# Two blocks of a transformer and a state space model on one core: the norms' root, reciprocal and spread in two halves of 64 columns

## What is computed

```python
def layer_norm(x, g, b):                       # four times: n = 0, 1, 2, 3
    mu = jnp.mean(xf, axis=-1, keepdims=True)
    var = jnp.mean(jnp.square(xf - mu), axis=-1, keepdims=True)
    return (xf - mu) * lax.rsqrt(var + LN_EPS) * g + b

def rmsnorm(x, g):                             # three times: n = 4, 5, 6
    return xf * lax.rsqrt(jnp.mean(xf * xf, axis=-1, keepdims=True) + RMS_EPS) * g

for i in range(2):                             # first block
    ...                                        # attention and retention, both gated
    x = layer_norm(ALPHA * x + merged @ w_out[i], ...)             # n = 0, 2
    x = layer_norm(ALPHA * x + conv_glu_ffn(x) + sigmoid(x @ w_ple_gate[i]) * (p[i] @ w_ple_proj[i]), ...)   # n = 1, 3
u = rmsnorm(x, norm_mix) @ w_in                # second block, n = 4
h = x + mixed(u) @ w_out
h = h + swiglu(rmsnorm(h, norm_ffn))           # n = 5
out = rmsnorm(h, norm_final)                   # n = 6
```

## Time and profile before

| | us |
|---|---|
| median of three runs | 2319.66 |
| lowest and highest | 2319.19, 2320.61 |
| the profiled execution, its own time | 2319.28 |
| its span in the trace | 2317.4 |
| TensorE (PE) busy in the span | 2287.2 (99%) |
| VectorE (DVE), ScalarE (ACT), GpSimd (POOL) busy | 962.9, 973.4, 1149.2 |

### The profile page before, as it was taken

The page is one execution under the profiler, slowest core; times in us unless marked ns, Lnnn a source line. Parts: engine busy times, 40 slices in busy tenths (PEclk is TensorE's granted clock), DMA queues, the critical chain, the costliest instruction groups (busy, mean ns, idle before and its releaser), DMA issues.

```text
span 2317.4 us, 32473 instructions
## 1 busy us (share of the span) xinstructions
PE 2287.2 (99%) x11672; PEld 1890.9 (82%) x11672; DVE 962.9 (42%) x1611; ACT 973.4 (42%) x1372; POOL 1149.2 (50%) x702
## 2 busy tenths in 40 slices
PE   8999999999999999999999999999999999999998
PEld 7888888888888887888888888888888777888886
DVE  6355343344444204453553353334376774222201
ACT  5444443244555325444453243555512534443321
POOL 3433334578995455333334465444455666444452
PEclk9999999999999999999999999999999999999999
DMA  5222223322223422222222323233333213233321
GB/s 208 77 67 88 79 80 101 100 85 93 91 93 106 135 92 84 70 88 79 78 83 91 100 83 100 91 100 100 100 103 107 65 38 109 91 100 100 99 92 55
DMA packets 61284, 214.18 MB, mean 92 GB/s; under 512 B 7200, under 2 KB 7456, under 8 KB 61216
## 3 DMA queue, kind: packets, MB, share of 16 engines
q1 hardware_dynamic: 58336, 205.10, 27.9%
q10 hardware_dynamic: 2880, 8.15, 1.1%
HBM read 211.13 MB, written 2.10 MB: 92 GB/s over the span
## 4 chain that ended last, share of the span: by engine, by line
PE 94%; DVE 3%; POOL 1%; ACT 1%; issue 1%; DMA 0%; DVEq 0%; ACTq 0%
PE psum L825 85%; PE psum L853 2%; PE psum L854 2%; PE psum L858 2%; PE psum L956 1%; PE psum L944 1%; PE psum L923 1%; POOL run L774 1%; PE psum L1223 0%; DVE states L2241 0%; PE psum L1012 0%; PE psum L1049 0%; DVE pr L1886 0%; POOL run L780 0%; POOL u_all L783 0%
## 5 line engine op out<-in xcount | busy, mean ns | idle before, releaser
L459 POOL TENSOR_TENSOR w_lo<-stage,w_hi 128x1024 fp32r<-128x1024 f32 x378 | 926.3, 2459 | 1070.7 <-ACT w_hi L1369 1055.8
L825 PE MATMUL psum<-xh,w_hi 128*128 128x512 f32 x1712 | 671.2, 392 | 0.7 <-DVE scaled L2366 0.7
L825 PE MATMUL psum<-xl,w_hi 128*128 128x512 f32 x1712 | 666.9, 390 | 0.0
L825 PE MATMUL psum<-xh,w_lo 128*128 128x512 f32 x1712 | 666.4, 389 | 0.0
L1369 ACT ACTIVATE w_hi<-stage 128x1024 fp32r<-128x1024 f32 x377 | 396.4, 1052 | 379.1 <-PE psum L825 377.6
L825 PEld LDWEIGHTS psum<-xh,w_hi 128*128 128x128 f32 x1712 | 321.3, 188 | 71.9 <-issue 2.4
L825 PEld LDWEIGHTS psum<-xh,w_lo 128*128 128x128 f32 x1712 | 321.4, 188 | 67.3
L825 PEld LDWEIGHTS psum<-xl,w_hi 128*128 128x128 f32 x1712 | 321.5, 188 | 65.0
L825 PE MATMUL psum<-g_hi,w_hi 128*128 128x512 f32 x528 | 206.2, 391 | 0.0
L825 PE MATMUL psum<-g_hi,w_lo 128*128 128x512 f32 x528 | 205.4, 389 | 0.0
L825 PE MATMUL psum<-g_lo,w_hi 128*128 128x512 f32 x528 | 205.4, 389 | 0.0
(11 more groups left out here) (399 smaller groups left out, 3359.3 us busy)
## 6 DMA issues: line engine op xcount, KB each, us to landing
stage<-in_w SPq DMA_DIRECT2D x379, 512.0 KB, 3.5
bias_raw<-in_bias ACTq DMA_DIRECT2D x8, 384.0 KB, 3.0
z<-in_x SPq DMA_DIRECT2D x3, 512.0 KB, 8.0
out_x<-out_t SPq DMA_DIRECT2D x3, 512.0 KB, 2.7
p_raw<-in_p ACTq DMA_DIRECT2D x2, 512.0 KB, 3.4
masks_raw<-in_masks SPq DMA_DIRECT2D x1, 576.0 KB, 11.1
masks_raw<-in_masks ACTq DMA_DIRECT2D x1, 576.0 KB, 4.6
z<-in_x SPq DMA_DIRECT2D x2, 256.0 KB, 5.5
```

The lines of the kernel that those rows point to most:

```text
L459: pool.tensor_tensor(w_lo[s][:, :, :], stage[s][:, :, :], w_hi[s][:, :, :].bitcast(F32), ALU.subtract).then_inc(lo_done, 1)
L825: mm = pe.matmul(dst, lhs[i], rhs[j], start=start and n == 0, stop=stop and n == 2)
```

## The change

The root, the reciprocal and the spread of every norm are cut into two halves of 64 columns. The semaphores `lstd` and `lrstd` count two steps a norm instead of one. `rstd_spread` still counts once, behind the second half: half h of each of the four groups lies at columns 128*i + 64*h, so the first tile needs both halves. On VectorE the order in a layer norm becomes `shift(0)`, `scale(0)`, `shift(1)`, `scale(1)`, `shift(2)`, `shift(3)`, `scale(2)`, `shift(4)`, `scale(3)` and so on as before.

```diff
+            def spread_halves(n, dst, rs):
+
+                for h in range(2):
+                    pe.wait_ge(lrstd, 2 * n + h + 1)
+                    for i in range(4):
+                        mm = pe.matmul(dst[:, i * P + 64 * h:i * P + 64 * h + 64], pick[:, i, :], rs[:, 64 * h:64 * h + 64],
+                                       start=True, stop=True)
+                mm.then_inc(rstd_spread, 1)
+
             def spread_scale(n):
-                ln_spread(R_BANK, rstd[:, 0:P], (lrstd, n + 1), rstd_spread)
+                spread_halves(n, R_BANK, rstd)
...
             def spread(n, rs):
 
-                pe.wait_ge(lrstd, n + 1)
-                for i in range(4):
-                    mm = pe.matmul(S_BANK[0][:, i * P:(i + 1) * P], pick[:, i, :], rs[:, 0:P], start=True, stop=True)
-                mm.then_inc(rstd_spread, 1)
+                spread_halves(n, S_BANK[0], rs)
...
-                act.activation(rstd[:, 0:P], rstd[:, 3 * P:4 * P], ACT.Sqrt, bias=ln_eps[:, :]).then_inc(lstd, 1)
+                for h in range(2):
+                    act.activation(rstd[:, 64 * h:64 * h + 64], rstd[:, 3 * P + 64 * h:3 * P + 64 * h + 64], ACT.Sqrt, bias=ln_eps[:, :])\
+                        .then_inc(lstd, 1)
...
-                act.activation(dst[:, 0:P], S_BANK[1][:, 0:P], ACT.Sqrt, bias=rms_eps[:, :]).then_inc(lstd, 1)
+                for h in range(2):
+                    act.activation(dst[:, 64 * h:64 * h + 64], S_BANK[1][:, 64 * h:64 * h + 64], ACT.Sqrt, bias=rms_eps[:, :])\
+                        .then_inc(lstd, 1)
...
+            def invert_root(n, rs):
+
+                for h in range(2):
+                    dve.wait_ge(lstd, 2 * n + h + 1)
+                    dve.reciprocal(rs[:, 64 * h:64 * h + 64], rs[:, 64 * h:64 * h + 64]).then_inc(lrstd, 1)
+
...
-                dve.wait_ge(lstd, n + 1)
-                dve.reciprocal(rstd[:, 0:P], rstd[:, 0:P]).then_inc(lrstd, 1)
+                invert_root(n, rstd)
...
                 shift(0)
-                shift(1)
                 for k in range(KT):
                     scale(k)
-                    if k + 2 < KT:
-                        shift(k + 2)
+                    for later in ((1,), (2, 3))[k] if k < 2 else (k + 2,):
+                        if later < KT:
+                            shift(later)
                     if to_mixer and k >= lag:
                         mixer_low(k - lag)
```

More of the change, by code:

```diff
@@ L2140, in last_norm @@
             def last_norm(n):
-                dve.wait_ge(lstd, n + 1)
-                dve.reciprocal(rstd_3[:, 0:P], rstd_3[:, 0:P]).then_inc(lrstd, 1)
+                invert_root(n, rstd_3)
                 dve.wait_ge(rstd_spread, n + 1)
@@ L2262, in mixer @@
                 n0 = MIX * 2
-                dve.wait_ge(lstd, n0 + 1)
-                dve.reciprocal(rstd_1[:, :], rstd_1[:, :]).then_inc(lrstd, 1)
+                invert_root(n0 + 1 - 1, rstd_1)
                 dve.wait_ge(rstd_spread, n0 + 1)
@@ L2357, in mixer @@
                 scaled_low(KT - 1)
-                dve.wait_ge(lstd, n0 + 2)
-                dve.reciprocal(rstd_2[:, 0:P], rstd_2[:, 0:P]).then_inc(lrstd, 1)
+                invert_root(n0 + 2 - 1, rstd_2)
                 dve.wait_ge(rstd_spread, n0 + 2)
```

## The result

| | before | after |
|---|---|---|
| median, us | 2319.66 | 2327.91 |
| lowest and highest, us (seven runs each) | 2319.19, 2320.61 | 2327.21, 2330.26 |
| the profiled execution, us | 2319.28 | 2327.93 |
| its span, us | 2317.4 | 2326.0 |

The change makes the kernel slower by 8.25 us, a ratio of 1.0036 (95% interval 1.0027 to 1.0046). Slower was forecast, with 6.15 us instead of 8.25. The 2319.66 of the kernel before is the median of seven runs, not of three.

A forecast was written before the change was run, and what follows sets the result against it. TensorE, busy 99% of the span, was taken to bound the kernel. Terms 2.2 + 0.5 + 1.45 + 0.4 + 0.85 + 0.75 = 6.15 us on 2319.28 gave 2325.4 us, range 2321.5 to 2328.

The forecast's parts named there:

- n = 1: Norm 1: spread starts 0.45 earlier, lasts 0.85 longer, second scaling adds 0.1, moved `shift(1)` free; +0.5 us.
- n = 3: Norm 3: start unchanged, spread ends 0.85 us later, moved `shift(1)` adds 0.60 to VectorE's chain; +1.45 us.
- n = 0 and 2: Norms 0 and 2: no wait to gain; TensorE +0.85 and about 0.25 from later low parts; +1.1 us each.
- The price of a pass: TensorE's spread: a pass stays at 0.106 us, set by its weight load; eight more cost 0.85 us a norm.
- The gain of the halves: Root and reciprocal: first half ready 0.45 us earlier; the second is never waited for.
- The term for GpSimd's low parts: Norms 0 and 2: GpSimd's low parts, without slack at tile 3, add about 0.25 us beyond TensorE's 0.85.
- VectorE's delay from tile 2 on: Norms 0 and 2: VectorE is 0.5 + 0.6 + 0.1 = 1.2 us later from tile 2 on.
- n = 6: Norm 6: +0.4 us at full clock, +0.75 if half of the sixteen passes run at half clock.
- The sign of being wrong: Forecast is wrong if clock levels in n = 1 and 6 change, or passes come faster than every 0.09 us.
- Rival C: Clock stays full in n = 1 and 6, 2323.8 us, chance 0.16; or falls in n = 3 or 4, 2326.9, 0.05.
- Rival B: All spreads: 64-column passes take half as long, sum 0, no change at 2319.3 us; chance 0.15.
- rival D: VectorE, four norms: moved subtraction lets first scaling start up to 0.6 us earlier; about 2317 with half-length passes; chance 0.07.

The follow-up runs named there:

- experiment 3: Kernel before with only VectorE's new order, no halves: 2321.29 us, ratio 1.0009.
- experiment 5: Kernel after with each half's spread cut once more, into 32 passes of 32 columns a norm: 2344.94 us, ratio 1.0112.
- experiment 6: Kernel after with VectorE's old order and the whole 128-column spread done twice, root and reciprocal still in halves: 2326.88 us, ratio 1.0032.
- experiment 4: Kernel after with the spread whole again and VectorE's old order, only root and reciprocal in halves: 2319.36 us, ratio 1.0002.
- experiment 8: Kernel before with filler matmuls, results unused, in TensorE's idle time in n = 1, 3 and 6: 2319.69 us, ratio 1.0001.
- experiment 2: Kernel after with only VectorE's old order restored, halves and half spreads kept: 2325.78 us, ratio 1.0029.
- experiment 7: Kernel after with filler matmuls, results unused, in TensorE's idle time in n = 1, 3 and 6: 2329.62 us, ratio 1.0037.
- experiment 1: Kernel after with only the spread whole again, halves of root and reciprocal and VectorE's new order kept: 2321.00 us, ratio 1.0008.

## Why the prediction was right in direction and short in size

The step that failed is that of n = 1: it put the moved `shift(1)` at nothing, because "TensorE is late there, at half clock". The runs show 0.73 us for the new order there (experiment 3), 0.6 of it the moved subtraction, since GpSimd's low parts and not the slow matmuls end the stage; with 0.2 more from a slow stretch that came later, the term of +0.5 measured 1.32. Next to it the terms of n = 3 (+1.45, measured 2.09) and of n = 0 and 2 (+1.1 each, measured 1.36 and 1.26) were too small.

- **The price of a pass**, which decided the sign, was right: 0.85 us for eight more passes was forecast from the weight loads, 0.89 was measured at n = 0 and 0.85 at n = 5, and experiments 5 and 6 show that columns do not count down to 32. The Trainium skill ("TensorE: Matmul & The Clock Gate", section "Back-to-back issue gap") gives about 60 cycles a matmul at 1 to 64 columns; here the distance from start to start stays at 0.112 us, about 269 cycles of 2.4 GHz, at 32 and 64 columns, so with a 128x128 f32 weight load ahead of each pass that figure does not hold.
- **The gain of the halves** was right: TensorE's wait in n = 1 fell by 0.46, and n = 4 cost 0.46 against 0.4. ScalarE's and VectorE's additional instructions cost nothing (experiment 4).
- **n = 0 and 2, +1.1 each**: measured 1.36 and 1.26. The term for GpSimd's low parts was 0.25 and is 0.4 to 0.5. VectorE's delay from tile 2 on was nearly right, 1.27 against 1.2. The step that fell short is behind it: 1.2 less TensorE's 0.85 is 0.35, of which the sum kept 0.25, as if GpSimd could make up 0.1. It makes up nothing: its last low part is 1.26 later, and the stage follows it.
- **n = 1, +0.5**: measured 1.32, the largest miss. The step that failed is "it delays tile 2, but TensorE is late there, at half clock". I had read the low parts as the limit for n = 0, where a weight load waited, and not here, where the slow matmuls hid the waits; but the stage ends with the same low parts, at the same 1.26 a tile. The moved subtraction costs 0.73 here (experiment 3), with the 0.1 of the second scaling that the forecast had. That and the spread's 0.39 are the 1.12 of the table. The other 0.20 comes from the slow stretch, which was put at no change. The half clock, which looked like a cost of the kernel before, cost it nothing (4 and 8).
- **n = 3, +1.45**: measured 2.09. The two named terms were right, 0.84 and 0.60. What was missing is 0.12 at the second scaling and 0.53 for one low part that started with an operation of GpSimd. The Trainium skill ("SBUF — State Buffer", section "SBUF: two separate sides") says that VectorE, when it reads two operands from SBUF, and GpSimd take one pair of ports in turn, each for a whole instruction. The row at 1816.15 agrees with it in kind: 1.27 us is 0.53 more than the usual 0.74. In size it is less than the 0.73 that GpSimd's operation, as the profile shows it, still had to run. No run was made to test the collision, but the low parts of the ten traces show that the two engines hold each other up, and the kernel before had it as well (1.15 us in its first low part, 0.41 more than 0.74). That ports are the reason stands in the Trainium skill alone; no run shows it.
- **n = 6, +0.75**: measured 1.04. The clock fell 0.65 us into the sixteen passes instead of half way. How near the forecast came was luck: over the traces this stage lies between 0.51 below and 4.58 above the kernel before, as the clock falls. The sign of being wrong that the prediction names, other levels of the clock in n = 1 and 6, did show: the slow stretch of n = 1 came later, and in n = 6 most of the sixteen passes were slow.
- **Rival C** had a part of 0.16 below the line and is refuted in the form given: full clock in n = 1 gives back 0.14 after the change, not 0.8. Its other form, a fall elsewhere, is real: falls in n = 3 cost about 1 us in experiments 2, 4 and 6, and falls behind n = 4 cost 1.6 to 3.3 in 5, 7 and 8.
- **Rival B** and **rival D** are refuted (experiments 5 and 6; experiment 3). The price at which B was to decide was worked out wrongly: sixteen passes of 0.09 us save 0.26 a norm, 1.8 in all, not 1.15, and 6.15 less 1.15 would be 5.0, not 4.9. The line of 4.6 us is met at 0.092 a pass, so "about 0.09" stands.

The missing 2.1 us is thus mostly n = 1 (0.8), n = 3 (0.65), n = 0 and 2 (0.4) and n = 6 (0.3). These shares are of the profiled span.

No version beat the kernel before. The two that equal it, experiments 4 and 8, differ from it by less than a run's spread.

## To carry to other kernels

Cutting a small matmul along its columns in order to start earlier multiplies weight loads; it pays only if the head start exceeds the additional passes, here 0.45 against 0.85 us, and only where TensorE waits at all. Before calling an instruction's delay free because its consumer is slow, look for the next chain of nearly the same length: here GpSimd's low parts stood right behind the slow matmuls. And an instruction moved from the time before a wait to the time behind it costs up to its full duration on every chain that starts at that wait: 0.73 us in n = 1, but 0.42 and 0.44 in n = 0 and 2, where the first scaling could start 0.3 earlier in exchange (experiment 3).

Two changes to a kernel in which two chains end close together do not add up. In n = 3 the one was 1.79 us, the other 1.02, both together 2.09.

## What was not expected of the hardware

- The place where the granted clock falls differs between kernels that differ little. In n = 3 it stayed full in the kernel before and in experiments 1, 7 and 8, and fell to half in 2 to 6 and in the kernel after. Such a fall cost nothing in the kernel after (experiment 7 without it is no shorter in n = 3), 0.96 us in experiment 4, where TensorE's sum of squares then came late, and a fall behind n = 4 cost 3.2 us in experiment 7. With one profile of each kernel it is not shown how much of this belongs to the kernel and how much to the execution.
- With fillers the clock was at 1.00 in n = 1 and n = 3, and it fell behind n = 4 (experiments 7 and 8). That the fillers held it is not shown: n = 1 was at 1.00 without them in experiments 4 and 6, and n = 3 in the kernel before. The sum was no gain: 2319.69 against 2319.25.
- At half clock the passes lie about 0.214 us apart instead of 0.112, at 128 columns (n = 6 before), 64 (n = 6 after) and 32 (n = 6 in experiment 5). What bounds them scales with TensorE's clock.
- VectorE's low part and GpSimd's operation of 128x256 hold each other up when they start nearly together: one of the two then takes up to 1.33 or 1.36 us instead of 0.74. In all but one of the cases in which VectorE started 0.6 us or more behind, it lost nothing.
